# Input stage of a hybrid GLA and differential-attention step: row blocks in pairs, two feature tiles in a bank, first weight tile by pieces

## The reference

```
def rmsnorm(x, g):
    xf = x.astype(F32)
    y = xf * lax.rsqrt(jnp.mean(xf * xf, axis=-1, keepdims=True) + EPS)
    return (y * g.astype(F32)).astype(x.dtype)
...
    xn = rmsnorm(x, attn_norm_g)
    proj = xn @ w_in
    gq, gk, gv, gg, glr, dq, dk, dv = jnp.split(proj, splits, axis=-1)
```

## Time and profile before

| | us |
|---|---|
| median of 3 runs | 1993.65 |
| the three runs | 1991.92, 1993.65, 1996.19 |
| the profiled execution | 1993.0 |
| its span, first to last instruction | 1991.4 |
| mean granted TensorE clock | 0.971 |

### The profile page before, as it was taken

The page is one execution under the profiler, slowest core; times in us unless marked ns, Lnnn a source line. Parts: engine busy times, 40 slices in busy tenths (PEclk is TensorE's granted clock), DMA queues, the critical chain, the costliest instruction groups (busy, mean ns, idle before and its releaser), DMA issues. The chain is left out here.

```text
span 1991.4 us, 35136 instructions
## 1 busy us (share of the span) xinstructions
PE 1851.9 (93%) x13458; PEld 1715.6 (86%) x13458; DVE 941.0 (47%) x1323; ACT 615.4 (31%) x1171; POOL 355.1 (18%) x366
## 2 busy tenths in 40 slices
PE   4999999985899999977999999999999999997998
PEld 4999999873666666657989999999999999997897
DVE  4223743454777777764343333333424424336443
ACT  4113322643555565643321111111111111113320
POOL 1112331001233333341111101100110110105110
PEclk9999999877999999998999999999999999999899
DMA  4323551307999999973112111111111111110221
GB/s 144 99 77 88 133 132 54 108 5 227 317 352 344 350 355 356 336 233 120 45 30 64 44 43 48 38 54 43 33 54 43 33 54 50 46 43 11 87 66 45
DMA packets 201608, 239.11 MB, mean 120 GB/s; under 512 B 15443, under 2 KB 142373, under 8 KB 201445
## 3 DMA queue, kind: packets, MB, share of 16 engines
q1 hardware_dynamic: 180964, 169.75, 27.5%
q0 software_dynamic: 20480, 67.13, 10.0%
HBM read 215.44 MB, written 16.91 MB: 117 GB/s over the span
## 5 line engine op out<-in xcount | busy, mean ns | idle before, releaser
L150 PE MATMUL psum<-h_hi,w_hi 128*128 128x364 f32 x1248 | 278.8, 332 | 2.7 <-issue 2.7
L150 PE MATMUL psum<-h_lo,w_hi 128*128 128x364 f32 x1248 | 276.3, 330 | 0.0
L150 PE MATMUL psum<-h_hi,w_lo 128*128 128x364 f32 x1248 | 275.2, 328 | 0.0
L2171 ACT ACTIVATE w_hi<-w_raw 128x1024 fp32r<-128x1024 f32 x66 | 68.8, 1059 | 587.2 <-PE psum L150 566.3
L150 PEld LDWEIGHTS psum<-h_hi,w_hi 128*128 128x128 f32 x1248 | 215.4, 189 | 4.8 <-issue 4.1
L150 PEld LDWEIGHTS psum<-h_lo,w_hi 128*128 128x128 f32 x1248 | 217.1, 189 | 0.0
L150 PEld LDWEIGHTS psum<-h_hi,w_lo 128*128 128x128 f32 x1248 | 216.7, 188 | 0.0
L1243 POOL DMA_DIRECT2D dec_v<-in_cache_v x256 | 137.5, 537 | 400.9 <-issue 277.1
L150 PE MATMUL psum<-x_hi,w_hi 128*128 128x364 f32 x792 | 188.7, 347 | 9.7 <-DVE x_lo L2004 5.8
L2147 POOL TENSOR_TENSOR w_raw<-w_raw,gains 128x1024 f32<-128x1024 f32 x42 | 80.4, 1915 | 650.4 <-DMA w_raw<-in_w_ffn_gate 352.0
L150 PE MATMUL psum<-x_hi,w_lo 128*128 128x364 f32 x792 | 176.1, 331 | 0.0
(11 more groups left out here) (257 smaller groups left out, 2724.3 us busy)
## 6 DMA issues: line engine op xcount, KB each, us to landing
dec_k<-in_cache_k SPq DMA_DIRECT2D x256, 256.0 KB, 5.5
dec_v<-in_cache_v POOLq DMA_DIRECT2D x256, 256.0 KB, 5.4
w_raw<-in_w_in SPq DMA_DIRECT2D x25, 512.0 KB, 3.9
w_raw<-in_w_ffn_gate SPq DMA_DIRECT2D x22, 512.0 KB, 3.8
w_raw<-in_w_ffn_up SPq DMA_DIRECT2D x22, 512.0 KB, 3.8
w_raw<-in_w_ffn_down SPq DMA_DIRECT2D x22, 512.0 KB, 3.7
feat_swap<-feat_n SPq DMA_DIRECT2D x32, 136.5 KB, 2.4
x_in<-in_x_prompt SPq DMA_DIRECT2D x4, 1024.0 KB, 8.5
```

Source lines behind the costliest of these rows:

```text
L150: ins = pe.matmul(out[:, c, 0:SPAN], w(k), x(k)[:, c * SPAN:c * SPAN + SPAN], start=n == 0 and w is whi and x is xhi, stop=n == len(ks) - ...
L2171: act.activation(m.whi[:, slot], m.raw[:, u], ACT.Copy).then_inc(s["w_hi"], 1)
```

## The change

The groups are now five: blocks 0 and 1, 2 and 3, 4 and 5, 6 and 7, and the sample. A fill holds two feature tiles of a pair (2 x 256 columns), and for the sample four feature tiles (4 x 64 columns), so there are 4 fills in each pair and 2 in the sample, 18 in all. The number of transposes is the same (64 and 8), and a fill of a pair still has 512 columns. Squares all go to `dense[1]`, so each waits for the one before. The order on ACT and DVE is interleaved: the roots and the scaling of the next pair stand ahead of the copies of the pair before. PE turns the four pairs, then runs the first weight tile in pieces, one span after the other (24 matmuls each), and turns the sample between the first and the second piece. The second piece waits for 12 fills, the third for all 18.

```
-    groups = [(0, 4), (4, 8), (8, 9)]
+    groups = [(0, 2), (2, 4), (4, 6), (6, 8), (8, 9)]
...
-    XT = 3 * KT
+    fills = [(g, i) for g in range(5) for i in range(4 if g < 4 else 2)]
+    XT = len(fills)
+    first_of = [fills.index((g, 0)) for g in range(5)]
+
+    def fill(n):
+        g, i = fills[n]
+        (a, b), per = groups[g], 2 if g < 4 else 4
+        return a, b, range(per * i, per * i + per), (b - a) * P if g < 4 else NS
...
@@ ACT
+            def roots(g):
+                a, b = groups[g]
                 rows = tokens_of(a)
+                act.wait_ge(x_ins[g], 16)
                 for j in range(a, b):
-                    if j % 2 == 0:
-                        act.wait_ge(x_ins[j // 2], 16)
-                    if j >= 2:
-                        act.wait_ge(x_squared, j - 1)
-                    act.activation(dense[j % 2][0:rows, 0:2, :]...
+                    if j:
+                        act.wait_ge(x_squared, j)
+                    act.activation(dense[1][0:rows, 0:2, :]...
...
+            roots(0)
+            roots(1)
+            take_hi(0)
+            roots(2)
+            take_hi(1)
+            roots(3)
+            take_hi(2)
+            hi(0, 0, True)
+            roots(4)
+            take_hi(3)
+            hi(1, 1, True)
+            take_hi(4)
@@ PE
+            def first_tile():
+                pe.wait_ge(w_lo, 1)
+                for c, g in ((0, 2), (1, 3), (2, 5)):
+                    pe.wait_ge(taken, first_of[g] if g < 5 else XT)
+                    for k in range(KT):
+                        for w, x in ((m.whi, m.xhi), (m.whi, m.xlo), (m.wlo, m.xhi)):
+                            ins = pe.matmul(dense[0][:, c, 0:SPAN], w[:, 0, k, :], x[:, k, c * SPAN:c * SPAN + SPAN],
+                                            start=k == 0 and w is m.whi and x is m.xhi, stop=k == KT - 1 and w is m.wlo)
+                    if c == 0:
+                        turn_x(4)
+                ins.then_inc(product_done, 1)
...
-            pe.wait_ge(taken, XT)
-            dense_tile(0, 0, first=True)
+            for g in range(4):
+                turn_x(g)
+            first_tile()
             dense_tile(1, 1, v_turn(0, 0), first=True)
@@ DVE
+            norm_x(0)
+            norm_x(1)
+            take_lo(0)
+            norm_x(2)
+            take_lo(1)
+            norm_x(3)
+            take_lo(2)
+            lo(0, 0)
+            norm_x(4)
+            take_lo(3)
+            lo(1, 1)
+            take_lo(4)
```

More of the change, by code:

```diff
@@ L203, in input_projection, with fill_bank, fill_cols, fills_of @@
     rsx = m.small[:, 32:48]
-    groups = [(0, 4), (4, 8), (8, 9)]
+    groups = [(0, 2), (2, 4), (4, 6), (6, 8), (8, 9)]
     thirds = [(0, 3), (3, 6), (6, 9)]
     NT = 25
-    XT = 3 * KT
+    fills = [(g, i) for g in range(5) for i in range(4 if g < 4 else 2)]
[5 more added lines that the diff above has]
+        return a, b, range(per * i, per * i + per), (b - a) * P if g < 4 else NS
+    def fill_bank(n):
+        a, b, ks, w = fill(n)
+        return x_banks[n % 4][:, 0:len(ks) * w].rearrange("p (k t) -> p k t", t=w)
+    def fill_cols(x, n):
+        a, b, ks, w = fill(n)
+        return x[:, ks[0]:ks[0] + len(ks), a * P:a * P + w]
+    def fills_of(g):
+        return [n for n in range(XT) if fills[n][0] == g]
     w_dram = io["w_in"].rearrange("o (k p) n -> p (o k) n", p=P)
@@ L383, in hi, with take_hi @@
                 act.activation(m.whi[:, slot], m.raw[:, slot], ACT.Copy).then_inc(w_hi, 1)
[L385 to L390, removed]
-                    act.wait_ge(filled, n + 1)
-                    act.activation(m.xhi[:, k, c0:c0 + cn], x_banks[n % 4][:, 0:cn], ACT.Copy).then_inc(x_hi, 1)
+            def take_hi(g):
+                for n in fills_of(g):
+                    act.wait_ge(filled, n + 1)
+                    act.activation(fill_cols(m.xhi, n), fill_bank(n), ACT.Copy).then_inc(x_hi, 1)
+            roots(0)
[10 more added lines that the diff above has]
+            take_hi(4)
             with act.Fori(0, 4) as i:
@@ L474, in _, with turn_x @@
             pe.wait_ge(consts_in, 16)
[L475 to L479, removed]
+            def turn_x(g):
+                rows = tokens_of(groups[g][0])
+                pe.wait_ge(x_normed, groups[g][1])
+                for n in fills_of(g):
+                    a, b, ks, w = fill(n)
                     if n >= 4:
                         pe.wait_ge(taken, n - 3)
-                    for j in range(a, b):
-                        ins = pe.transpose(x_banks[n % 4][:, (j - a) * P:(j - a) * P + rows],
-                                           m.x_in[0:rows, j, k * P:k * P + P], ident[0:rows, 0:rows])
+                    for i, k in enumerate(ks):
+                        for j in range(a, b):
+                            ins = pe.transpose(fill_bank(n)[:, i, (j - a) * P:(j - a) * P + rows],
+                                               m.x_in[0:rows, j, k * P:k * P + P], ident[0:rows, 0:rows])
                     ins.then_inc(filled, 1)
+            def first_tile():
[9 more added lines that the diff above has]
+                ins.then_inc(product_done, 1)
             def dense_tile(s, u, between=(), first=False):
@@ L560, in _, with norm_x @@
             dve.memset(f32(m.xlo[:, :, NP + NS:T]), 0.0)
-            for g, (a, b) in enumerate(groups):
+            def norm_x(g):
+                a, b = groups[g]
                 rows = tokens_of(a)
```

15 lines of the change are left out of this document (5 added, 10 removed).

## The result

The changed kernel took 1978.04 us (median of 4 runs, 1974.68 to 1979.66) against 1992.81 for the kernel before (4 runs, 1991.92 to 1996.19): a ratio of 0.9925, 95% interval 0.991 to 0.994, or 14.8 us less. Ratios and intervals are given as they were recorded; differences in us are those of the two medians, so the two need not agree to the last digit.

A forecast was written before the change was run, and what follows sets the result against it. The input stage, up to tile 1's start, was taken to bound the time: 27.8 + 12.0 + 0.5 = 40.3 against 53.63, 13.3 less 0.6 for handoffs, so 1993.65 - 12.7 = 1981.0 us, range 1977.5 to 1987.0.

The forecast's parts named there:

- given back later: Rival, stages after the input: meeting half clock once more returns 5 us (1986, chance 0.11); twice leaves nothing measurable.
- The chain to tile 0: Input stage on ACT, DVE, POOL and PE: tile 0 starts at about 27.8 us instead of 40.15.
- second branch: PE's transposes of pair 3 at the slow 0.91 us a fill: ready at 28.4, where tile 0 then starts.
- first branch: PE's transposes of pair 3 at the faster pace: ready at 27.0, waiting for `w_lo` at 27.6; tile 0 about 27.8.
- fast start: Tile 0 begins at full clock because transposes alone bring the faster pace; tile 1 at 40.3, total 1981.0, chance 0.50.
- fast case: Input stage with faster transposes and tile 0 at full clock: 1981.0 us, by itself reaching from 1979 to 1983.
- second case: Rival, half pace at tile 0's start: 1.5 us lost there, tile 1 at 43.0, total 1983 to 1984.5, chance 0.28.
- The tile with the sample inside: First weight tile: 72 matmuls in 12.0 us plus 0.5 for the sample's 8 transposes, its wait hidden.
- The collision of POOL and DVE: Input stage of the kernel before: five DVE scalings take 6.68 us, 3.4 expected, 3.3 lost where they meet POOL.
- One bank serialises: Rival, 24 matmuls adding into one bank wait for each other: 2005 (chance 0.04), or 1992.7 with loads hidden.
- The sum: Start of tile 1: 27.8 + 12.0 + 0.5 = 40.3 against 53.63, a gain of 13.3, or 12.7 after a deduction.
- handoffs: Some ten short passes between engines on the chain, counted at nothing: 0.6 us taken off the 13.3 gain.

The follow-up runs named there:

- e_warm_16: Changed kernel with 16 extra, unread transposes on PE between the second and third pair; 1979.63 us in a single execution.
- e_warm_48: Changed kernel with 48 extra, unread transposes on PE between the second and third pair; 1972.02 us in a single execution.
- e_before_again: The kernel before, unaltered, run again for a second profile; no total of its own is given, tile 1 started at 54.91 us.
- e_changed_again: The changed kernel, unaltered, in five more rounds beside the kernel before; 1977.09 us, ratio 0.9918 to the kernel before.
- e_one_bank: Changed kernel with the span loop outermost in every dense tile with nothing between its matmuls; 1978.08 us, ratio 0.9926 to the kernel before.
- e_two_squares: Changed kernel with squares going to two buffers in turn again, each waiting only for the one before last; 1983.58 us in a single execution.
- e_pool_late: Kernel before, with POOL waiting until all nine blocks are scaled before touching the first weight tile; ratio 0.9978, 3.9 us less.
- e_early: Changed kernel with the first tile's weights made before pair 2 is taken and its first piece run earlier; 1978.18 us, ratio 0.9932 to the kernel before.
- e_warm: Changed kernel with 32 extra, unread transposes on PE between the second and third pair; 1992.85 us in one execution, 1992.73 over 10 runs.
- e_pieces: Kernel before with only the first tile run in pieces, the sample turned after the first piece; ratio 0.998, 4.9 us less.

## Why the prediction was right, step by step

- **What bounds the kernel.** Right: all of the stage's gain arrived in the total, and no later stage gave any of it back (in the table each later stage of the changed kernel agrees with the kernel before within the scatter of two profiles). The rival "given back later" has fallen.
- **The chain to tile 0.** 27.8 us was forecast, 27.73 measured (27.4 to 27.9 in every kernel with this order). By its links: first scaling 8.9 against 8.85, fills of pair 2 taken by 26.4 against 26.14, `w_lo` by 27.6 against 27.28. Each came up to 0.3 us earlier, and PE's slow transposes took that up: they had the pace of the forecast's second branch, but started 0.2 earlier than it said and took 3.28 us, not 3.65. So 27.8 came out of two deviations that cancelled. By the first branch with its links as measured, tile 0 would have started near 27.4, as it did in e_warm_16 and e_warm_48 (27.44, 27.38); by the second as forecast, at 28.4.
- **The clock.** The forecast took the fast start since transposes alone had brought the faster pace before. That they do is borne out. In the changed kernel the rise came at 27.8, behind transposes since 24.5, though with the tile's first weight load (27.73) just begun. In e_before_again the granted clock rose from 0.50 to 1.00 at 31.8, in the middle of a row of transposes (PE timeline, then the busy time by stretch):

```profile
26.12 6.48 PE L483 MATMUL psum<-consts,x_in 128*128 128x128 f32 x32 [8.01 <-DVE x_lo L580]
```

```profile
31.00:32.00 1.00, 1.00 (x8) 1.00 (x6) 0.74 (x2) 1.00 (x2) 0.00 (x0) 0.58 0.00 0
32.00:33.00 1.00, 0.60 (x6) 0.36 (x4) 1.00 (x2) 1.00 (x3) 0.00 (x0) 1.00 0.00 0
```

  And in e_warm_48, where PE had only transposes up to tile 0 (the 16 of pair 2 took 1.91 us, 0.12 each), tile 0 ran at 1.00 from its second matmul on (0.33 us each). Here the trace disagrees with the Trainium skill ("TensorE: Matmul & The Clock Gate", Part 4: PE-mode transpose), by which the full clock doesn't engage in transpose mode. What the forecast missed is PE's idle stretch of 3.5 us before pair 2, though it follows from its own schedule: eight fills at 0.91 from 10.4 on end by 17.7, and pair 2 is not scaled before 19. Its fast case took the transposes of pair 3 at the faster pace, and they were slow. The tile met the full clock after all, by a margin of no more than the last transpose. That was luck: of the four profiles with this order on PE up to tile 0, only this one has the clock back there; in e_changed_again and e_one_bank the first three or four matmuls ran at half clock (tile 1 at 41.04 and 41.06), in e_two_squares the first eight or nine (41.88). The slow start thus cost between 0 and about 1 us, where the sum had nothing and the second case 1.5.
- **The tile with the sample inside.** 12.0 + 0.5 forecast, 12.8 measured. The 0.3 are the sample's: from the last load of the first piece at 31.53 to the first of the second at 32.59 are 1.06 us, 0.9 more than one step. The third piece waited for nothing, as forecast: DVE was done with the sample at 33.6 (33.5 forecast).
- **The collision of POOL and DVE.** Priced at 3.3 us, measured 3.28 in e_pool_late. In the profile after the change 0.1 us is left of it on DVE; in e_two_squares it was 0.7.
- **One bank serialises.** Fallen by e_one_bank, and by the pace of 0.166 us in the changed kernel's own first piece.
- **The sum.** 40.3 was forecast for tile 1, 40.52 measured: a stage gain of 13.1 against 13.3. The 0.6 us then taken off for handoffs were not needed in this profile; with tile 1 at 41.04, as in the second one, they were. In the stage the gain is 0.4 more than the 12.7 of the forecast. The other 1.7 up to 14.8 lie behind tile 1, where the forecast had nothing: the first pair of profiles has 2.2 us there, the second pair none. Against 1981.0 the measured 1978.04 is 3.0 lower: some 0.8 because the median of the kernel before came out lower than the one shown, 0.4 from the stage and 1.7 from behind tile 1. No step named that last part, and the range took the result in by only 0.5 us.

## What to carry to other kernels

When an engine's queue is a chain of small steps in fixed order, write out each engine's schedule from the durations in the trace, instruction by instruction: here that gave each link of the chain to 0.3 us, and the start of the first tile, where the deviations cancelled, to 0.1. Ask of each step that is moved forward what buffer it frees and which engine that wakes: the early weights of e_early brought POOL onto DVE's ports. And compare the sequencer's issue waits in distant loops before a difference is explained: 32 instructions at the start of a program cost 15 us in a loop that begins 1000 us later.

## What the runs showed of the hardware that I had not expected

- The same loop costs 718.4, 721.2, 722.3 or 738.1 us, by 48, 0, 16 or 32 extra transposes in front of it. The difference is time in which TensorE stands on issue at the loop's jump back (none, 2.0, 2.3, 10.0 us), with matmuls at half clock behind the long stops. In the kernel with 48 the instruction queue moved nothing for two rounds of the loop, in the others 16 to 18 packets of 16 KB.
- TensorE's clock in the input stage, by kernel: the changed kernel's PE was idle for 3.52 us up to 19.68 and the granted clock read 0.50 from 21 us; e_warm's was idle for 2.46 up to 24.66 and it read 0.50 from 26; e_pieces' was idle for 2.41 up to 34.31 and it read 0.50 from 34, still within that stretch. e_warm_16's was idle for 2.62 up to 24.61 and it stayed at 1.00. The same kernel met it differently in two executions (tile 1 at 53.63 and 54.91 before, at 40.52 and 41.04 after), so a tile that starts just behind such a stretch has a scatter of about 1 us of its own. A rule from the length of the idle stretch alone does not fit these rows.
